# Expert weights loaded in blocks of two experts with 8 KB runs, and multiplied in pairs of blocks

## Chip, core and metric

One core of one Trainium2 chip runs the program. The metric is the device time of one execution in microseconds. The core has five engines with queues of their own: TensorE (PE), VectorE (DVE), ScalarE (ACT), GpSimd (POOL) and SyncE (SP); 16 DMA engines move data between HBM and the on-chip memory. In this kernel SyncE issues all loads of weights. "Records" of a matmul are lines of the trace; one float32 matmul leaves two.

## What is computed

Two blocks of a network over 256 tokens of 1024 features, all in float32. The first block has a mixer (convolution and gated linear attention) and then a mixture of 32 experts; the second block has attention, pooling, a state-space branch and a feed-forward part. The change lies in the mixture of experts of the first block:

```python
def hierarchical_moe(h, w_rg, b_rg, w_re, b_re, w1, w3, w2):
    t = h.reshape(B * S, D)
    lg = (t @ w_rg + b_rg).astype(jnp.float32)             # 4 groups of experts
    ...                                                      # best group, its two best experts, weights
    comb = jnp.einsum("tk,tke->te", w, jax.nn.one_hot(eid, N_EXPERTS, dtype=jnp.float32))
    y = jnp.zeros((B * S, D), jnp.float32)
    for e in range(N_EXPERTS):
        hid = jax.nn.silu(t @ w1[e]) * (t @ w3[e])
        y = y + comb[:, e:e + 1] * (hid @ w2[e]).astype(jnp.float32)
    return y
```

`w1` and `w3` are [32, 1024, 512], `w2` is [32, 512, 1024]: together 201 MB of float32, each read once.

## The kernel before

**Stages.** The program goes through the first block (to about 363 us), the experts (to about 884 us) and the second block. In the stages around the experts the matmuls of L554 and L551 run with split operands made by VectorE and ScalarE; they aren't touched.

**Experts.** They are taken four at a time, eight "quads". For each expert at most `CAP` = 32 tokens are gathered, so the four experts of a quad fill the 128 columns of a tile. The routing (VectorE, with two small steps of ScalarE) makes `hot`, a matrix of ones and zeros; `gather_tokens` (TensorE L803, VectorE L1566) multiplies `uT` (tokens x features) by it and gives `xg`, features on the partitions, in 8 tiles of 128 features. If an expert had more than 32 tokens, a general path (`If_ne`) would run afterwards; it leaves no lines in this trace.

**Blocks and slots.** The weights of a quad come in 12 blocks of 2.097 MB (16 KB on each partition): `wide_of(quad, i)` gives the slot of block i. Blocks 0 to 3 are w1, 4 to 7 are w3, each block two tiles of 128 features for all four experts; blocks 8 to 11 are w2, one tile of 128 hidden features each. There are eight slots (`NW`), three in `above` and five in `arena`, used in turn over all 96 blocks. A row of w1 or w3 is 512 elements, and tiles are taken as `(t p)`: partition p of tile t is feature 128 t + p, so that one contiguous run in HBM is one row, 2 KB (4 KB for w2).

**SyncE.** `expert(quad, i)` (L2463) waits until the slot's former block has been multiplied (`up_made` or `down_made` of that block) and issues four DMAs of 512 KB, one for each expert. The first eight blocks wait for ends of earlier work instead (`out_v`, `scaled_v`). The DMAs of all 96 blocks stand in one row in the queue; the loads of the second block of the network come behind them and wait for `sent[7]`, the end of the last quad on TensorE.

**TensorE, for each quad.** Up products (L825): for w1 and then w3, for each of four blocks, wait for the block (`wide_in`), 2 tiles x 4 experts = 8 matmuls, each expert in its own 32 rows of the bank; `up_made` is raised after each block. Then the gather for the next quad (L803), two transposes of the send weights (L836), four transposes of `hid` (L840), the down products (L849: for each of four blocks 2 x 4 = 8 matmuls, `down_made` after each), and the products that send the results back to the tokens (L862).

**VectorE and ScalarE.** ScalarE makes `s1` = silu of the first bank and copies the transposed `hid` out; VectorE multiplies `s1` by the second bank to `hid`. Ahead of the stage ScalarE copies the turned `u` into `uT` in four pieces (L2135, recorded as L1912).

Of the kernel before, what the change touches and what calls it, by code (L numbers as in the profile page):

```python
# [137 lines left out]
def build(nc, T, out, scratch):  # L138
    ctx = ExitStack()
    with ctx:  # L140
# [274 lines left out]
        w1v, w3v, w2v = (T[n][0].rearrange("(j e) (t p) n -> j p e t n", e=4, p=P) for n in ("w1", "w3", "w2"))  # L415

        def wide_of(quad, i):

            n = 12 * quad + i
            return n % NW, wides[n % NW].rearrange("p (e t n) -> p e t n", e=4, t=2 if i < 8 else 1), n  # L420
# [90 lines left out]
        def tensor_program(e):  # L511
# [298 lines left out]
            for quad in range(8):  # L810
# [5 lines left out]
                for wn in range(2):  # L816
                    bank = take(wn, (silu_a, hid_v)[wn], quad)
                    for th in range(4):
                        s, slot, n = wide_of(quad, 4 * wn + th)
                        e.wait_ge(*wide_in[s][n])  # L820
                        if wn == 0 and th % 2 == 0:
                            e.wait_ge(*gathered[quad, th // 2])
                        for k in range(2):
                            for x in range(4):
                                ins = e.matmul(bank[32 * x:32 * x + 32, :], xg[:, i, 2 * th + k, 32 * x:32 * x + 32],  # L825
                                               slot[:, x, k, :], start=th == 0 and k == 0, stop=th == 3 and k == 1,
                                               skip_group_check=True)
                        ins.then_inc(*up_made.up((quad, 4 * wn + th)))
# [15 lines left out]
                for k in range(4):  # L844
                    s, slot, n = wide_of(quad, 8 + k)
                    e.wait_ge(*wide_in[s][n])
                    for c in range(2):
                        for x in range(4):
                            ins = e.matmul(ob[c][32 * x:32 * x + 32, :], hidT[:, i, k, 32 * x:32 * x + 32],  # L849
                                           slot[:, x, 0, 512 * c:512 * c + 512], start=k == 0, stop=k == 3, skip_group_check=True)  # L850
                    ins.then_inc(*down_made.up((quad, k)))
# [298 lines left out]
        def vector_program(e):  # L1150
            state = dict(split=0, made=0)

            def tt(o, a, b, f):
                return e.tensor_tensor(o, a, b, f)  # L1154
# [416 lines left out]
            for quad in range(8):  # L1571
# [14 lines left out]
                tt(hid, s1, banks[1][:, :], ALU.mult).then_inc(*hid_v.up(quad))  # L1586
# [321 lines left out]
        def scalar_program(e):  # L1908
# [223 lines left out]
            for tc in range(2):  # L2132
                for g in range(2):
                    e.wait_ge(*u_turned[tc, g])
                    act(uT[:, tc, 512 * g:512 * g + 512], bank_of(uT_out, (tc, g))[:, :], ACT.Copy).then_inc(*uT_out.up((tc, g)))  # L2135
# [230 lines left out]
        def sync_program(e):  # L2366
# [83 lines left out]
            def expert(quad, i):  # L2450
                s, slot, n = wide_of(quad, i)
                if n >= NW:
                    prior, pi = (n - NW) // 12, (n - NW) % 12
                    e.wait_ge(*(up_made[prior, pi] if pi < 8 else down_made[prior, pi - 8]))
                elif s < 4:
                    e.wait_ge(*out_v["w_out", 3])
                else:
                    e.wait_ge(*ada_sum[31])
                    e.wait_ge(*scaled_v[1, 6])
                    e.wait_ge(*scaled_a[1, 7])  # L2460
                src, at, kt = (w1v, 2 * i, 2) if i < 4 else (w3v, 2 * i - 8, 2) if i < 8 else (w2v, i - 8, 1)
                for x in range(4):
                    e.dma_start(slot[:, x, :, :], src[quad, :, x, at:at + kt, :]).then_inc(*wide_in[s].up(n, 16))  # L2463
# [128 lines left out]
```

## Time and profile before

| | us |
|---|---|
| median of 3 runs | 1522.9 (1517.42 to 1524.58) |
| profiled execution | 1524.56 |
| its span, first to last instruction | 1522.8 |
| TensorE busy | 1248.3 (82%) |
| VectorE busy | 676.4 (44%) |
| ScalarE busy | 454.5 (30%) |

The share of busy time of an engine is an average over stages that have different limits. The page also splits the span into 40 slices of 38 us with the GB/s that the DMA engines moved in each. The mean granted clock of TensorE is 0.892 of full speed (2.4 GHz; the other level is 1.2 GHz, shown as 0.5). A DMA share of 1 means that packets took all the time of 16 DMA engines; as the records of packets overlap a little, it can read 1.05.

### The profile page before, as it was taken

What the parts mean: (1) busy time and instruction counts of PE and PEld (TensorE: products, weight loads), DVE (VectorE), ACT (ScalarE), POOL (GpSimd) and SP (SyncE); (2) the same over time, 40 slices, a digit from 0 to 9 for tenths busy, and PEclk for the clock granted to TensorE, in tenths of its full rate; (3) what the DMA queues carried; (4) which work ended last, traced back from release to release, by engine and by line L of the source; (5) the groups of instructions that cost most, each with busy time, mean ns of one, the idle gap of its engine ahead of it and who ended that gap; (6) DMA issues with size and microseconds to landing.
All of it is one profiled execution on the core that took longest, in us unless ns stands there. A gap on an engine that the chain in (4) does not pass through costs nothing.

```text
span 1522.8 us, 20505 instructions
## 1 busy us (share of the span) xinstructions
PE 1248.3 (82%) x8742; PEld 970.9 (64%) x8742; DVE 676.4 (44%) x1137; ACT 454.5 (30%) x647; POOL 1.9 (0%) x15
## 2 busy tenths in 40 slices
PE   6889988698676566566757669999999989899998
PEld 3679987587432131221212149989998879899986
DVE  2546985453300000000000055355567777667975
ACT  1533341533100000000000044343444544455453
POOL 0000000000000000000000000000000000000000
PEclk8899989899697887987778689989999989999999
DMA  9686730587999999999999947444346334445652
GB/s 356 240 281 216 220 99 1 198 279 263 391 394 398 387 398 391 395 398 388 399 389 396 396 158 229 152 139 124 126 128 191 112 111 152 136 142 174 200 206 85
DMA packets 226568, 374.51 MB, mean 246 GB/s; under 512 B 8854, under 2 KB 121896, under 8 KB 226344
## 3 DMA queue, kind: packets, MB, share of 16 engines
q1 hardware_dynamic: 226304, 369.58, 68.6%
q0 software_dynamic: 144, 3.54, 0.7%
q8 instruction: 71, 1.16, 0.3%
q14 instruction: 25, 0.20, 0.0%
q10 hardware_dynamic: 24, 0.03, 0.0%
HBM read 372.03 MB, written 4.62 MB: 247 GB/s over the span
## 4 chain that ended last, share of the span: by engine, by line
PE 50%; SPq 22%; DVE 13%; DMA 8%; ACT 3%; issue 3%; DVEq 0%; ACTq 0%
PE bank L554 30%; SPq L2463 22%; DVE arena L1162 5%; DMA arena<-in_w 4%; PE bank L1131 4%; DVE fine L1154 4%; DMA above<-in_w 2%; DVE arena L1154 2%; PE bank L825 2%; ACT fine L1912 2%; DMA arena<-in_w_ada 2%; PE bank L551 2%; PE bank L582 1%; ACT arena L1912 1%; PE bank L751 1%
## 5 line engine op out<-in xcount | busy, mean ns | idle before, releaser
L554 PE MATMUL bank<-fine 128*128 128x256 f32 x4656 | 587.5, 289 | 34.9 <-DVE fine L1154 24.2
L554 PEld LDWEIGHTS bank<-fine 128*128 128x128 f32 x4656 | 577.6, 197 | 44.3 <-issue 33.9
L1154 DVE TENSOR_TENSOR fine<-arena,fine 128x1024 fp32r<-128x1024 f32 (+1 forms) x257 | 299.3, 1192 | 175.3 <-ACT fine L1912 165.9
L1912 ACT ACTIVATE fine<-arena 128x1024 fp32r<-128x1024 f32 (+2 forms) x279 | 267.0, 984 | 178.7 <-PE bank L554 106.7
L1912 ACT ACTIVATE arena<-bank 128x256 f32<-128x256 f32 (+2 forms) x161 | 73.5, 482 | 606.7 <-PE bank L836 194.2
L825 PE MATMUL bank<-arena 128*32 128x512 f32 x640 | 105.7, 798 | 76.0 <-DMA arena<-in_w 76.0
L1154 DVE TENSOR_TENSOR arena<-arena,bank 128x512 f32<-128x512 f32 x8 | 5.5, 689 | 299.6 <-PE bank L825 299.6
L825 PEld LDWEIGHTS bank<-arena 128*32 128x32 f32 x640 | 20.6, 129 | 154.8 <-DMA arena<-in_w 103.1
L1912 ACT ACTIVATE arena<-arena 128x512 f32<-128x512 f32 (+6 forms) x94 | 63.3, 702 | 171.1 <-DVE arena L1154 80.4
L1162 DVE SCALAR_TENSOR_TENSOR arena<-arena 128x256 f32<-128x256 f32 (+2 forms) x265 | 108.3, 481 | 1.2 <-ACT arena L1912 0.8
L825 PE MATMUL bank<-above,arena 128*32 128x512 f32 x384 | 61.7, 778 | 39.5 <-DMA above<-in_w 39.5
L1154 DVE TENSOR_TENSOR arena<-arena 128x512 f32<-128x512 f32 (+5 forms) x138 | 84.1, 633 | 8.6 <-ACT arena L1912 6.7
L1154 DVE TENSOR_TENSOR arena<-bank,arena 128x256 f32<-128x256 f32 (+6 forms) x88 | 36.0, 446 | 86.3 <-PE bank L594 17.0
L849 PE MATMUL bank<-arena 128*32 128x512 f32 x320 | 50.5, 768 | 27.7 <-DMA arena<-in_w 24.2
L825 PEld LDWEIGHTS bank<-above,arena 128*32 128x32 f32 x384 | 12.3, 127 | 86.3 <-DMA above<-in_w 48.1
L1131 PE MATMUL bank<-fine 128*128 128x512 f32 x264 | 60.3, 390 | 0.0
L1598 DVE COPY arena<-bank 128x512 f32<-128x512 f32 x8 | 5.5, 692 | 122.1 <-PE bank L849 122.1
L1131 PEld LDWEIGHTS bank<-fine 128*128 128x128 f32 x264 | 49.4, 188 | 10.7 <-DVE fine L1154 0.3
L849 PEld LDWEIGHTS bank<-arena 128*32 128x32 f32 x320 | 11.0, 131 | 62.1 <-DMA arena<-in_w 36.9
L551 PE MATMUL bank<-fine 128*128 128x256 f32 x384 | 47.1, 283 | 0.1
L551 PEld LDWEIGHTS bank<-fine 128*128 128x128 f32 x384 | 46.4, 192 | 0.3 <-issue 0.3
L803 PEld LDWEIGHTS bank<-arena 128*128 128x128 f32 x256 | 32.7, 211 | 11.7 <-issue 11.7
(160 smaller groups left out, 814.0 us busy)
## 6 DMA issues: line engine op xcount, KB each, us to landing
arena<-in_w SPq DMA_DIRECT2D x240, 512.0 KB, 11.7
above<-in_w SPq DMA_DIRECT2D x144, 512.0 KB, 11.4
arena<-in_w_in SPq DMA_DIRECT2D x62, 1024.0 KB, 5.3
arena<-in_w_ada SPq DMA_DIRECT2D x24, 1024.0 KB, 7.7
arena<-in_ffn_w_up SPq DMA_DIRECT2D x22, 1024.0 KB, 5.1
arena<-in_ffn_w_down SPq DMA_DIRECT2D x11, 1024.0 KB, 4.9
arena<-in_w_ada_f SPq DMA_DIRECT2D x8, 1024.0 KB, 10.6
arena<-in_w_gla_o SPq DMA_DIRECT2D x4, 1024.0 KB, 8.5
```

The lines of the kernel that those rows point to most:

```text
L551: ins = e.matmul(o, x[:, kt, j * P:j * P + P], w[:, k, :], start=start, stop=stop, skip_group_check=True)
L554: ins = e.matmul(o, w[:, k, j * P:j * P + P], x[:, kt, :], start=start, stop=stop, skip_group_check=True)
L582: ins = e.matmul(bank[32 * k:32 * k + 32, :], cact[:, kt:kt + 1].to_broadcast([P, 32]), slot[:, k, :], start=f % 2 == 0, stop=f % 2 == 1, ...
L751: ins = e.matmul(bank[:, j * 256:j * 256 + 256], w_pw[m // 4][:, k, (m % 4) * P:(m % 4) * P + P], sig[:, k, :], start=k == 0, stop=k == 3)
L803: ins = e.matmul(bank[:, j * P:j * P + P], uT[:, tc, k * P:k * P + P], hot2[:, tc, quad * P:quad * P + P], start=tc == 0, stop=tc == 1)
L825: ins = e.matmul(bank[32 * x:32 * x + 32, :], xg[:, i, 2 * th + k, 32 * x:32 * x + 32], slot[:, x, k, :], start=th == 0 and k == 0, stop=t ...
L849: ins = e.matmul(ob[c][32 * x:32 * x + 32, :], hidT[:, i, k, 32 * x:32 * x + 32], slot[:, x, 0, 512 * c:512 * c + 512], start=k == 0, stop ...
L1131: ins = e.matmul(obs[tc][c][:, :], x, w[:, cs], start=n == i == 0, stop=n == 21 and i == 2, skip_group_check=True)
L1154: return e.tensor_tensor(o, a, b, f)
L1162: return e.scalar_tensor_tensor(out=o, in0=a, scalar=s, in1=b, op0=f1, op1=f2)
L1912: return e.activation(o, i, f, bias=bias, scale=scale)
L2463: e.dma_start(slot[:, x, :, :], src[quad, :, x, at:at + kt, :]).then_inc(*wide_in[s].up(n, 16))
```

## The change

The tiles of w1, w3 and w2 are taken as `(p t)`: partition p of tile t is feature 8 p + t for w1 and w3, and hidden feature 4 p + t for w2. Then successive tiles of one partition are neighbours in HBM. A block holds two experts instead of four, and four tiles instead of two (two instead of one for w2), so that a run is 4 x 2 KB or 2 x 4 KB, 8 KB in both cases. The block is as large as before, and there are as many of them; SyncE issues two DMAs of 1 MB for each, one for each expert. The products of four tiles for all four experts need two blocks now, so TensorE waits for both blocks of a pair, runs 16 matmuls and raises `up_made` (or `down_made`) once. Slots are freed likewise, both after the pair. The number of matmuls and their shapes are unchanged.

The features have to be in the same order in the other operand: ScalarE writes `uT` permuted, reading the bank with a stride of 8 elements, and VectorE writes `hid` permuted with a stride of 128 elements.

```diff
--- before.py
+++ after.py
@@ -412,12 +412,14 @@
 
         GENERAL = [i for i in range(NW) if i != 4]
         NG = len(GENERAL)
-        w1v, w3v, w2v = (T[n][0].rearrange("(j e) (t p) n -> j p e t n", e=4, p=P) for n in ("w1", "w3", "w2"))
+        w1v, w3v, w2v = (T[n][0].rearrange("(j e) (p t) n -> j p e t n", e=4, p=P) for n in ("w1", "w3", "w2"))
 
         def wide_of(quad, i):
 
+
+
             n = 12 * quad + i
-            return n % NW, wides[n % NW].rearrange("p (e t n) -> p e t n", e=4, t=2 if i < 8 else 1), n
+            return n % NW, wides[n % NW].rearrange("p (e t n) -> p e t n", e=2, t=4 if i < 8 else 2), n
 
         def general_of(e0, i):
             n = 96 + 3 * e0 + i
@@ -815,17 +817,20 @@
                     e.reg_load(reg, idxb[0:1, 16:17])
                 for wn in range(2):
                     bank = take(wn, (silu_a, hid_v)[wn], quad)
-                    for th in range(4):
-                        s, slot, n = wide_of(quad, 4 * wn + th)
-                        e.wait_ge(*wide_in[s][n])
-                        if wn == 0 and th % 2 == 0:
-                            e.wait_ge(*gathered[quad, th // 2])
-                        for k in range(2):
+                    for th in range(2):
+                        slots = []
+                        for pair in range(2):
+                            s, slot, n = wide_of(quad, 4 * wn + 2 * th + pair)
+                            e.wait_ge(*wide_in[s][n])
+                            slots.append(slot)
+                        if wn == 0:
+                            e.wait_ge(*gathered[quad, th])
+                        for k in range(4):
                             for x in range(4):
-                                ins = e.matmul(bank[32 * x:32 * x + 32, :], xg[:, i, 2 * th + k, 32 * x:32 * x + 32],
-                                               slot[:, x, k, :], start=th == 0 and k == 0, stop=th == 3 and k == 1,
+                                ins = e.matmul(bank[32 * x:32 * x + 32, :], xg[:, i, 4 * th + k, 32 * x:32 * x + 32],
+                                               slots[x // 2][:, x % 2, k, :], start=th == 0 and k == 0, stop=th == 1 and k == 3,
                                                skip_group_check=True)
-                        ins.then_inc(*up_made.up((quad, 4 * wn + th)))
+                        ins.then_inc(*up_made.up((quad, 4 * wn + 2 * th + 1)))
                 if quad == 0:
                     ada_to_mod(15)
                 if quad < 7:
@@ -841,14 +846,19 @@
                 ins.then_inc(*hid_turned.up(quad))
                 ob = [take(2 + n, (expert_a, expert_v)[n], ("ye", quad)) for n in range(2)]
                 e.wait_ge(*hidT_out[quad])
-                for k in range(4):
-                    s, slot, n = wide_of(quad, 8 + k)
-                    e.wait_ge(*wide_in[s][n])
-                    for c in range(2):
-                        for x in range(4):
-                            ins = e.matmul(ob[c][32 * x:32 * x + 32, :], hidT[:, i, k, 32 * x:32 * x + 32],
-                                           slot[:, x, 0, 512 * c:512 * c + 512], start=k == 0, stop=k == 3, skip_group_check=True)
-                    ins.then_inc(*down_made.up((quad, k)))
+                for th in range(2):
+                    slots = []
+                    for pair in range(2):
+                        s, slot, n = wide_of(quad, 8 + 2 * th + pair)
+                        e.wait_ge(*wide_in[s][n])
+                        slots.append(slot)
+                    for k in range(2):
+                        for c in range(2):
+                            for x in range(4):
+                                ins = e.matmul(ob[c][32 * x:32 * x + 32, :], hidT[:, i, 2 * th + k, 32 * x:32 * x + 32],
+                                               slots[x // 2][:, x % 2, k, 512 * c:512 * c + 512], start=th == k == 0,
+                                               stop=th == k == 1, skip_group_check=True)
+                    ins.then_inc(*down_made.up((quad, 2 * th + 1)))
                 e.wait_ge(*send_out[quad])
                 for m in range(8):
                     if quad == 0 and m % 2 == 0:
@@ -1583,7 +1593,8 @@
                 e.wait_ge(*up_made[quad, 7])
                 if quad:
                     e.wait_ge(*hid_turned[quad - 1])
-                tt(hid, s1, banks[1][:, :], ALU.mult).then_inc(*hid_v.up(quad))
+                tt(hid.rearrange("p (t a) -> p a t", t=4), shaped(s1, P, 4), shaped(banks[1][:, :], P, 4), ALU.mult).then_inc(
+                    *hid_v.up(quad))
                 if quad < 7:
                     gather_tokens(quad + 1)
                 e.wait_ge(*route["hot"])
@@ -2132,7 +2143,8 @@
             for tc in range(2):
                 for g in range(2):
                     e.wait_ge(*u_turned[tc, g])
-                    act(uT[:, tc, 512 * g:512 * g + 512], bank_of(uT_out, (tc, g))[:, :], ACT.Copy).then_inc(*uT_out.up((tc, g)))
+                    act(shaped(uT[:, tc, :], 8, P)[:, :, 64 * g:64 * g + 64],
+                        bank_of(uT_out, (tc, g))[:, :].rearrange("p (a t) -> p t a", t=8), ACT.Copy).then_inc(*uT_out.up((tc, g)))
             for tc in range(2):
                 t = rt[:, 128 * tc:128 * tc + 128]
                 e.wait_ge(*route["ex", tc])
@@ -2451,16 +2463,16 @@
                 s, slot, n = wide_of(quad, i)
                 if n >= NW:
                     prior, pi = (n - NW) // 12, (n - NW) % 12
-                    e.wait_ge(*(up_made[prior, pi] if pi < 8 else down_made[prior, pi - 8]))
+                    e.wait_ge(*(up_made[prior, pi | 1] if pi < 8 else down_made[prior, pi - 8 | 1]))
                 elif s < 4:
                     e.wait_ge(*out_v["w_out", 3])
                 else:
                     e.wait_ge(*ada_sum[31])
                     e.wait_ge(*scaled_v[1, 6])
                     e.wait_ge(*scaled_a[1, 7])
-                src, at, kt = (w1v, 2 * i, 2) if i < 4 else (w3v, 2 * i - 8, 2) if i < 8 else (w2v, i - 8, 1)
-                for x in range(4):
-                    e.dma_start(slot[:, x, :, :], src[quad, :, x, at:at + kt, :]).then_inc(*wide_in[s].up(n, 16))
+                src, at, kt = (w1v, 4 * (i // 2), 4) if i < 4 else (w3v, 4 * (i // 2) - 8, 4) if i < 8 else (w2v, 2 * (i // 2) - 8, 2)
+                for x in range(2):
+                    e.dma_start(slot[:, x, :, :], src[quad, :, 2 * (i % 2) + x, at:at + kt, :]).then_inc(*wide_in[s].up(n, 16))
 
             for quad in range(8):
                 if quad == 4:
```

On TensorE, at the start of quad 0 (`wide_in0` to `wide_in7` are the arrivals in the eight slots, `gathered` is `xg`), there stood before:

```order
L825 MATMUL bank<-above,arena 32x512 [waits gathered,wide_in0,pieces_out_by_vector]
L825 MATMUL bank<-above,arena 32x512 x7
L825 MATMUL bank<-above,arena 32x512 [waits wide_in1]
L825 MATMUL bank<-above,arena 32x512 x7
L825 MATMUL bank<-above,arena 32x512 [waits gathered,wide_in2]
L825 MATMUL bank<-above,arena 32x512 x7
L825 MATMUL bank<-arena 32x512 [waits wide_in3]
L825 MATMUL bank<-arena 32x512 x7
```

and now:

```order
L830 MATMUL bank<-above,arena 32x512 [waits wide_in1,gathered,wide_in0,pieces_out_by_vector]
L830 MATMUL bank<-above,arena 32x512 x15
L830 MATMUL bank<-above,arena 32x512 [waits gathered,wide_in3,wide_in2]
L830 MATMUL bank<-above,arena 32x512
L830 MATMUL bank<-arena 32x512 x2
L830 MATMUL bank<-above,arena 32x512 x2
```

Eight matmuls behind one arrival have become sixteen behind two; the second pair has one block in `above` and one in `arena`, so its matmuls alternate between them.

On SyncE, at blocks 6 to 9 (`expert_up` is `up_made`), before:

```order
L2463 DMA arena<-in_w 128x2x512 [waits scaled_by_scalar,scaled_by_vector,ada_sum]
L2463 DMA arena<-in_w 128x2x512 x3
L2463 DMA above<-in_w 128x1024 [waits expert_up]
L2463 DMA above<-in_w 128x1024 x3
L2463 DMA above<-in_w 128x1024 [waits expert_up]
```

and now:

```order
L2475 DMA arena<-in_w 128x2048 [waits scaled_by_scalar,scaled_by_vector,ada_sum]
L2475 DMA arena<-in_w 128x2048
L2475 DMA above<-in_w 128x2048 [waits expert_up]
L2475 DMA above<-in_w 128x2048
L2475 DMA above<-in_w 128x2048 [waits expert_up]
```

Four DMAs of a block have become two, each with one contiguous row of 2048 elements for a partition; the waits stand in the same places, and that of block 8 is for the first pair instead of the first block.

## Rows read from the trace of the kernel before

**Rows 1.** The page, 40 slices of the span: GB/s.

```profile
GB/s 356 240 281 216 220 99 1 198 279 263 391 394 398 387 398 391 395 398 388 399 389 396 396 158 229 152 139 124 126 128 191 112 111 152 136 142 174 200 206 85
```

**Rows 2.** Windows in the expert stage; the header names the columns.

```profile
core 0: us, PE busy (x) PEld busy (x) DVE busy (x) ACT busy (x) POOL busy (x), PEclk, DMA share, GB/s
366.00:408.00 42.00, 25.79 (x139) 22.49 (x141) 20.52 (x81) 9.46 (x19) 0.00 (x0) 0.63 1.05 388
...
440.00:470.00 30.00, 19.04 (x105) 4.53 (x104) 0.00 (x0) 0.60 (x1) 0.00 (x0) 0.72 1.05 386
415.00:430.00 15.00, 12.90 (x114) 7.36 (x110) 3.09 (x8) 0.98 (x2) 0.00 (x0) 0.97 1.03 408
...
728.70:792.50 63.80, 42.62 (x247) 16.16 (x247) 3.09 (x5) 2.18 (x4) 0.00 (x0) 0.73 1.04 394
```

**Rows 3.** Waits, 360 to 890 us: total us, times, longest.

```profile
PE bank L825 <- DMA arena<-in_w: 76.0, 30, 3.6
...
PE bank L825 <- DMA above<-in_w: 39.5, 17, 3.9
```

**Rows 4.** Waits of SyncE over the whole span.

```profile
SPq L2463 <- PE bank L825: 22.8, 10, 7.6
```

**Rows 5.** Timeline, SyncE's issues at the start of the stage: start, us, what.

```profile
363.84 11.03 SPq L2463 DMA_DIRECT2D above<-in_w  x12
374.91 26.39 SPq L2463 DMA_DIRECT2D arena<-in_w  x20
408.96 5.57 SPq L2463 DMA_DIRECT2D above<-in_w  x12
```

**Rows 6.** Timeline, TensorE at the start of the stage.

```profile
401.33 5.71 PE L803 MATMUL bank<-arena 128*128 128x128 f32 x32 [3.54 <-issue]
406.97 5.36 PE L825 MATMUL bank<-above,arena 128*32 128x512 f32 x48
```

**Rows 7.** DMA view, 440 to 470 us (first factors): all packets.

```profile
DMA packets 6008, 11.59 MB, mean 386 GB/s; under 512 B 355, under 2 KB 355, under 8 KB 6007
```

**Rows 8.** DMA view, 415 to 430 us (second factors): all packets.

```profile
DMA packets 1675, 6.12 MB, mean 408 GB/s; under 512 B 184, under 2 KB 184, under 8 KB 1674
```

**Rows 9.** DMA view, 54 to 56 us: constants with rows of 5.25 KB, and others.

```profile
DMA packets 240, 0.82 MB, mean 412 GB/s; under 512 B 28, under 2 KB 69, under 8 KB 240
```

**Rows 10.** DMA view, 370 to 371 us: queue: packets, MB, share of 16 engines.

```profile
q14 instruction: 1, 0.01, 2.1%
```

**Rows 11.** DMA view, 158 to 169.5 us: the copy from scratch to scratch.

```profile
q0 software_dynamic: 139, 3.54, 94.5%
```

**Rows 12.** Chain of waits, 700 to 800 us: start, us, what.

```profile
728.67 2.82 PE bank L825 x16
...
792.50 1.97 PE bank L825 x16
```

**Rows 13.** Timeline, TensorE on two blocks of quad 4.

```profile
643.00 1.92 PE L825 MATMUL bank<-above,arena 128*32 128x512 f32 x16 [1.91 <-DMA above<-in_w]
648.43 3.64 PE L825 MATMUL bank<-arena 128*32 128x512 f32 x16 [3.51 <-DMA arena<-in_w]
```

**Rows 14.** Timeline, TensorE at the end of the stage.

```profile
882.05 1.93 PE L849 MATMUL bank<-arena 128*32 128x512 f32 x16 [1.77 <-DMA arena<-in_w]
884.78 3.69 PE L862 MATMUL bank<-arena 128*128 128x256 f32 x16 [0.81 <-ACT arena L1912]
```

**Rows 15.** Timeline, ScalarE: last of four copies to `uT`, and what follows.

```profile
387.14 0.60 ACT L1912 ACTIVATE arena<-bank 128x512 f32<-128x512 f32 x1 [0.26 <-PE bank L786]
387.76 1.28 ACT L2139 ACT_TABLE_LOAD   x1
```

**Rows 16.** The page: queue (packets, MB, share), issues (count, KB, us to landing).

```profile
q14 instruction: 25, 0.20, 0.0%
...
arena<-in_w SPq DMA_DIRECT2D x240, 512.0 KB, 11.7
...
arena<-in_consts SPq DMA_DIRECT2D x1, 672.0 KB, 10.8
```

## Prediction

> **What bounds the kernel now.** I read the slices of the page first, for the stretch in which the change lies. From about 380 to 870 us the slices stand at 387 to 399 GB/s [rows 1], the highest and flattest stretch of the program; the windows put the DMA share there at 1.03 to 1.05 of 16 engines, with VectorE and ScalarE almost idle and TensorE busy 42.6 of 63.8 us of one quad [rows 2]. This is the expert stage, and its 96 blocks of 2.097 MB are 201 MB. Second, the waits: what TensorE waits for in it is the DMA of the expert weights, some 3.5 us at a time [rows 3]. Third, whether the DMA queue ever waits for a free slot: SyncE waited 22.8 us in all on L825, in 10 waits, the longest 7.6 us [rows 4], and that longest one is the gap between the last issue of the first 32 (374.91 + 26.39 = 401.30) and 408.96 [rows 5]. So the stage is bound by the DMA engines, and the rest of the program (before 365 us and after 884 us) isn't touched, but for shifting.
>
> The period of a quad is 792.50 - 728.67 = 63.83 us in the chain [rows 12]. It has two speeds in it: 386 GB/s while first factors come in (runs of 2 KB) and 408 GB/s while second factors come in (runs of 4 KB) [rows 2]. All have 512 KB in a DMA [rows 16]; what differs is the run.
>
> **Cost of a packet.** From 440 to 470 us 6008 - 355 - 1 = 5652 packets of 2 KB moved [rows 7]: 30 us x 16 / 5652 = 84.9 ns each. From 415 to 430 us 1675 - 184 - 1 = 1490 packets of 4 KB moved [rows 8]: 161.1 ns each. A fixed part c and a part in proportion to the bytes give c = 2 x 84.9 - 161.1 = 8.7 ns, and for 8 KB 2 x 161.1 - 8.7 = 313.5 ns, if a run of 8 KB is one packet. A block is 64, 32 or 16 packets on each engine: 5.43, 5.16 and **5.02 us** (418 GB/s). Check of the old numbers: 8 x 5.43 + 4 x 5.16 = 64.1, against 63.83 in the chain. Nearest row above 4 KB: from 54 to 56 us, while constants with rows of 5.25 KB come in among others, the mean is 412 GB/s [rows 9, 16].
>
> The Trainium skill (DMA: Bandwidth & Descriptors, "Why small descriptors are slow (HBM only)") has a fixed overhead of about 3 cycles per packet, and under "Where 436 GB/s comes from" a ceiling of 435 GB/s. The 8.7 ns above are of that kind, and somewhat more than its 3 cycles at the 850 MHz that the section gives (an estimate of 3.5 ns); by the page's terms an 8 KB block would be about 4.88 us.
>
> **The change part by part.**
> - First factors, 64 blocks: 5.43 to 5.02 us each. Second factors, 32 blocks: 5.16 to 5.02 us. DMAs 384 to 192, so SyncE issues less; it wasn't the limit, since it issued 20 in 26.39 us [rows 5], 5.3 us for the four of a block, in step with a queue that was full. Worth nothing.
> - **The start takes part of it back.** Eight slots are filled while TensorE is still at the routing. The first issue is at 363.84 [rows 5], and from 366 on the rate is full [rows 2]; I take 365.2 as the start, 1.3 us from issue to flow. Before, eight blocks last to 365.2 + 8 x 5.43 = 408.6, and block 8 is issued at 408.96, when block 0 has been multiplied: no gap. The change fills the slots by 365.2 + 8 x 5.02 = 405.4, but L825 begins at 406.97 whatever the DMA does, since it follows the gather of L803 [rows 6] and that the routing. Now both blocks of a pair must be multiplied before a slot is free. 48 records take 5.36 us [rows 6], so 32 take 3.5 and SyncE can issue at about 410.7; data flow again at 412.0. The DMA idles from 405.4 to 412.0, and block 8 starts 412.0 - 408.7 = **3.3 us later** than before. What the faster transfer gained on blocks 0 to 7 is lost here.
> - Blocks 8 to 95: before 56 x 5.43 + 32 x 5.16 = 469.2 us, after 88 x 5.02 = 441.8 us: **27.4 us saved**.
> - Steady stage: the wait for a pair holds the even slot for one block longer, 5 us, and the work on a pair is 3.9 us at 2.4 GHz or 7.3 at 1.2 GHz (1.92 and 3.64 us for 16 records [rows 13]). When a pair has landed, three pairs are queued behind it, 30 us of transfers. TensorE's longest lag behind a landing, all at 1.2 GHz, comes after the last up pair: 7.3 of up, 5.7 of gather [rows 6], 3 of transposes (an estimate), twice 7.3 of down, 7.4 of L862 (twice the 3.69 of rows 14), then the next up pair, 7.3: 45 us after the one landing, and 15 after that of the next up pair, three pairs later. So the queue doesn't run dry: nothing.
> - **The end.** The last block of the stage lands at 882.05 and takes 1.93 us, then come the copies and L862 at 884.78 [rows 14]. Now the last two blocks are multiplied after the landing: 3.9 us at the high clock, 7.3 at the low one, so 1.9 to 5.4 us more. The clock before was mostly between (0.73 of full over a quad [rows 2]); I take the middle, **3.6 us**.
> - uT: four ScalarE copies of 0.60 us, the routing's exponentials right behind them [rows 15]; now they read PSUM with a stride of 8. The trace has no such shape for ScalarE. A gain is excluded, as they would wait for TensorE's transposes all the same; the other bound is twice as long, 4 x 0.60 less 3 x 0.26 of idle time between them = 1.6 us. I take 0, as the elements are as many. Later routing would push the start of L825 and so block 8.
> - hid on VectorE, 0.69 us, is written with a stride: hidden, since the down products wait for their blocks anyway.
>
> **Sum.** 27.4 - 3.3 - 3.6 = 20.5 us less. Against the profiled execution: 1524.6 (span 1522.8) to 1504.1. That execution lies 1.7 us above the median of 1522.9, so the median goes to **1502**.
>
> **Rivals.**
> 1. *No faster than the second factors' runs.* Either the hardware cuts 8 KB rows into 4 KB, or the memory side has its limit at about 408 GB/s. For it: no packet of 8 KB from SyncE is in the trace. Against: the 412 GB/s with rows of 5.25 KB [rows 9]. Then 88 x 5.16 = 454.1, 15.1 us saved, less 6.9: 8 us, **1515**. The skill (HBM Reference, "Specifications (TRN2)") gives about 358 GB/s as effective per core; with that as a cap there would be nothing to win from runs at all. It also says that a core streaming alone measures more, and the trace does: 386 and 408.
> 2. *Slower: a packet of 8 KB costs more than in proportion.* Its place is every block of the stage. Instruction packets have 0.20 MB in 25, 8 KB each [rows 16], and the one amid the stream took 2.1% of 16 us, 336 ns [rows 10]; and packets of 27 KB, copied within HBM, moved 3.54 MB in 94.5% of 11.5 us, 326 GB/s [rows 11]. At 336 ns a block is 5.38 us, 88 are 473.1, 3.9 more than before, and 6.9 on top: 10.8 us more, **1534**. It decides at (469.2 - 6.9) / 88 = 5.25 us a block, 328 ns a packet, 399 GB/s. Against: both are other kinds of transfer, and the first one's time has other packets of the same engine in it (packets of 2 KB overlap likewise: the shares add up to 1.05, not 1). Rows of 8 KB now lie 16 KB apart in HBM, which no row here shows.
> 3. *More than computed.* Without a fixed part at all, 4.88 us a block, and the high clock at the end: 469.2 - 429.4 - 3.3 - 1.9 = 34.6, **1488**.
> 4. *TensorE becomes the bound.* Now 42.6 us of 63.8 are busy at a clock of 0.73 [rows 2]. All at 1.2 GHz a quad is 12 x 3.64 + 5.7 + 7.4 + 3 = 59.8 us [rows 6, 13, 14], against 12 x 5.02 = 60.2 of DMA. It would need that clock in every quad, and then waits between the two could cost some 1 us a quad: about **1510**.
>
> **How the numbers follow.** Forecast 1502, chance 0.62, own range 1495 to 1510 (block 4.95 to 5.07 us, end 1.9 to 5.4, routing 0 to 1.6). Rival 1: 0.15; rival 2: 0.09; rival 3: 0.08; rival 4: 0.06. The range 1490 to 1518 takes in the forecast, rivals 1 and 4 and half of 3; left out are 2 and the rest of 3. A measurement of this kernel tells about 0.5%, 7.6 us, from no change. Rival 1 lies at that bound (1515.3), half of it on either side. Slower is rival 2; same is half of rival 1 and 0.02 of the others' edges: faster 0.81, same 0.10, slower 0.09.
>
> **What would show it.** In the profile after: windows within the stage at 415 to 420 GB/s, equal for first and second factors; quads 60.2 us apart; about 24,600 packets of 8 KB; SyncE's wait before block 8 up from 7.7 us to far more (its 16 DMAs are queued by 380 us), with 0 GB/s between about 406 and 412; L825 in groups of 32 records; the last block landing at about 857 and 3.9 to 7.3 us of work behind it. I'm wrong if the stage stays at 408 GB/s or lower, if L825 begins later than 407, or if the DMA rate falls in the middle of the stage, which would be slots held too long.

## The result

The change brings 1498.4 us (median of 4 runs, 1496.8 to 1502.8) against 1523.7 (4 runs): ratio 0.9847, interval 0.9813 to 0.9881. (Ratios come with 95% intervals; they are not the quotients of the medians shown.) The prediction was 1502, within 1490 to 1518. The profiled execution took 1498.0 us, its span 1496.2.

What answers to [rows 2], windows of the stage after the change (us, busy time of each engine with instructions, granted clock, DMA share, GB/s):

```profile
440.00:470.00 30.00, 16.95 (x98) 4.30 (x96) 0.00 (x0) 0.60 (x1) 0.00 (x0) 0.77 1.01 420
416.00:430.00 14.00, 11.71 (x102) 6.86 (x94) 3.46 (x8) 0.98 (x2) 0.00 (x0) 1.00 1.01 421
```

First factors (from 440 us; 386 GB/s before) and second factors (from 416 us; 408 before) come in at one rate. All packets from 440 to 470 us, to compare with [rows 7]:

```profile
DMA packets 1730, 12.61 MB, mean 420 GB/s; under 512 B 192, under 2 KB 192, under 8 KB 192
```

Taking off the 192 short packets, 16 for each DMA of the weights, and one packet of instructions leaves 1730 - 192 - 1 = 1537 packets of 8 KB: 30 x 16 / 1537 = 312.3 ns each. The sum had 313.5. So a row of 8 KB from HBM is one packet, and rival 1 is out.

The start of the stage, SyncE and TensorE, to compare with [rows 5, 6]:

```profile
361.45 3.36 SPq L2475 DMA_DIRECT2D above<-in_w  x6
364.86 13.84 SPq L2475 DMA_DIRECT2D arena<-in_w  x10
408.31 4.25 SPq L2475 DMA_DIRECT2D above<-in_w  x6
```

```profile
398.94 5.74 PE L805 MATMUL bank<-arena 128*128 128x128 f32 x32 [3.53 <-issue]
404.61 4.06 PE L830 MATMUL bank<-above,arena 128*32 128x512 f32 x34
```

The eight slots are all ordered by 378.7 us; then SyncE has nothing to do until 408.31. The windows show the gap that was forecast:

```profile
404.00:406.00 2.00, 2.00 (x23) 0.99 (x25) 0.69 (x1) 0.00 (x0) 0.00 (x0) 1.00 0.62 258
406.00:408.00 2.00, 2.00 (x24) 0.57 (x20) 0.00 (x0) 0.00 (x0) 0.00 (x0) 1.00 0.02 8
408.00:410.00 2.00, 2.00 (x24) 0.65 (x20) 0.00 (x0) 0.00 (x0) 0.00 (x0) 1.00 0.46 61
410.00:412.00 2.00, 2.00 (x24) 0.60 (x20) 0.00 (x0) 0.25 (x1) 0.00 (x0) 1.00 0.90 348
```

The DMA engines stand still for about 4 us, where 6.6 were forecast (405.4 to 412.0; why it is shorter stands below), because TensorE is still at the routing and then at the first pair. The end, to compare with [rows 14]:

```profile
851.91 6.12 PE L858 MATMUL bank<-arena 128*32 128x512 f32 x32 [6.26 <-DMA arena<-in_w]
858.84 3.48 PE L872 MATMUL bank<-arena 128*128 128x256 f32 x15 [0.81 <-ACT arena L1923]
```

32 records behind the last landing instead of 16, and most of them at 1.2 GHz: 6.12 us instead of 1.93.

SyncE's waits for slots, to compare with [rows 4]; the second row had no counterpart among those shown of before:

```profile
SPq L2475 <- PE bank L830: 73.6, 27, 29.6
...
SPq L2475 <- PE bank L858: 28.0, 11, 5.4
```

It waits 102 us instead of 23, and that costs nothing beyond the start, as the page's GB/s in 40 slices, to compare with [rows 1], stay at 420 or 421 through the middle:

```profile
GB/s 356 267 272 216 218 108 1 197 255 266 367 421 421 421 421 420 421 420 421 421 421 421 297 179 223 127 141 113 129 156 153 139 87 162 134 160 178 197 198 85
```

The queue just holds more. The page has 27.0 us from issue to landing where [rows 16] has 11.7:

```profile
arena<-in_w SPq DMA_DIRECT2D x120, 1024.0 KB, 27.0
above<-in_w SPq DMA_DIRECT2D x72, 1024.0 KB, 26.3
```

**Balance of the two profiled executions.** I count the stage from the first issue of expert weights to the first record of the products after the last block (L862 before, L872 now).

| | before | after | |
|---|---|---|---|
| program start to first issue | 363.84 | 361.45 | -2.4 |
| first issue to issue of block 8 | 45.12 | 46.86 | +1.7 |
| block 8's issue to last landing | 473.09 | 443.60 | -29.5 |
| last work and copies | 2.73 | 6.93 | +4.2 |
| from there to the end of the span | 638.0 | 637.4 | -0.7 |
| span | 1522.8 | 1496.2 | -26.6 |

The stage is 520.9 us before and 497.4 after, **23.5 us shorter**, where 20.5 were forecast; 3 us more lie where both programs do the same. (In another execution of the change, below, the first issue is at 364.54.)

### The profile page after: what moved, and what is told of

It reads as the page before. It is cut to its first block, busy times and chain, and to the rows that moved or that the text cites. A ratio compares the mean times of both kernels' runs of the same rounds, so it can differ in the third digit from the quotient of the medians.

```text
span 1496.2 us, 20337 instructions
## 1 busy us (share of the span) xinstructions
PE 1225.0 (82%) x8742; PEld 974.1 (65%) x8742; DVE 679.2 (45%) x1137; ACT 454.7 (30%) x647; POOL 1.9 (0%) x15
## 4 chain that ended last, share of the span: by engine, by line
PE 55%; DMA 20%; DVE 13%; SPq 5%; ACT 3%; issue 3%; DVEq 0%; ACTq 0%
PE bank L556 30%; DMA arena<-in_w 15%; DVE arena L1172 5%; SPq L2475 4%; PE bank L1141 4%; PE bank L830 4%; DMA above<-in_w 4%; DVE fine L1164 4%; DVE arena L1164 2%; ACT fine L1923 2%; PE bank L858 2%; DMA arena<-in_w_ada 2%; PE bank L553 2%; PE bank L584 1%; ACT arena L1923 1%
## 5 line engine op out<-in xcount | busy, mean ns | idle before, releaser
L830 PE MATMUL bank<-arena 128*32 128x512 f32 x640 | 122.0, 782 | 53.5 <-DMA arena<-in_w 28.8
L1164 DVE TENSOR_TENSOR arena<-arena,bank 128x512 f32<-128x512 f32 x8 | 8.4, 1055 | 277.6 <-PE bank L830 277.6
L830 PE MATMUL bank<-above,arena 128*32 128x512 f32 x384 | 82.5, 786 | 50.8 <-issue 17.9
L830 PEld LDWEIGHTS bank<-arena 128*32 128x32 f32 x640 | 31.0, 138 | 107.5 <-issue 107.5
L830 PEld LDWEIGHTS bank<-above,arena 128*32 128x32 f32 x384 | 21.1, 138 | 108.8 <-issue 108.7
L858 PE MATMUL bank<-arena 128*32 128x512 f32 x320 | 57.0, 742 | 21.7 <-DMA arena<-in_w 19.1
L858 PE MATMUL bank<-above,arena 128*32 128x512 f32 x192 | 34.1, 652 | 20.1 <-DMA arena<-in_w 16.7
L858 PEld LDWEIGHTS bank<-arena 128*32 128x32 f32 x320 | 14.6, 132 | 46.0 <-issue 46.0
```

Source lines behind the costliest of these rows:

```text
L830: ins = e.matmul(bank[32 * x:32 * x + 32, :], xg[:, i, 4 * th + k, 32 * x:32 * x + 32], slots[x // 2][:, x % 2, k, :], start=th == 0 and k ...
L858: ins = e.matmul(ob[c][32 * x:32 * x + 32, :], hidT[:, i, 2 * th + k, 32 * x:32 * x + 32], slots[x // 2][:, x % 2, k, 512 * c:512 * c + 51 ...
```

## Experiments

Each kernel was timed beside the kernel before on the same chip (medians of before 1523.5 to 1524.1), and the ratio is to those runs. "Stage" is counted as above, from each one's profile.

| | median us | ratio to before | stage us | GB/s, 440 to 470 us |
|---|---|---|---|---|
| before | 1523.7 | 1 | 520.9 | 386 |
| the change | 1498.4 | 0.9847 | 497.4 | 420 |
| a_pairs_2k | 1530.3 | 1.0038 [1.0024, 1.0052] | 525.7 | 387 |
| b_4k_single | 1508.4 | 0.9892 [0.9874, 0.9910] | 505.8 | 409 |
| d_16k | 1500.6 | 0.9848 [0.9832, 0.9865] | 497.7 | 427 |
| e_8k_halves | 1896.5 | 1.2473 [1.2402, 1.2544] | 886.9 | 227 |
| i_8k_interleaved | 1500.8 | 0.9856 [0.9834, 0.9877] | 497.9 | 419 |
| f_end | 1496.9 | 0.9832 [0.9814, 0.9849] | 494.3 | 421 |
| g_both | 1494.8 | 0.9808 [0.9794, 0.9822] | 493.2 | 421 |
| h_16k_both | 1487.7 | 0.9755 [0.9739, 0.9770] | 486.1 | 428 |
| j_change_again | 1500.0 | 0.9841 [0.9827, 0.9854] | 497.4 | 420 |
| k_both_again | 1493.7 | 0.9807 [0.9788, 0.9826] | 493.3 | 420 |

### Is it the run, or the pairs with their larger DMAs?

**a_pairs_2k**: the change with the old order of features.

```diff
-        w1v, w3v, w2v = (T[n][0].rearrange("(j e) (p t) n -> j p e t n", e=4, p=P) for n in ("w1", "w3", "w2"))
+        w1v, w3v, w2v = (T[n][0].rearrange("(j e) (t p) n -> j p e t n", e=4, p=P) for n in ("w1", "w3", "w2"))
...
-                    act(shaped(uT[:, tc, :], 8, P)[:, :, 64 * g:64 * g + 64],
-                        bank_of(uT_out, (tc, g))[:, :].rearrange("p (a t) -> p t a", t=8), ACT.Copy).then_inc(*uT_out.up((tc, g)))
+                    act(uT[:, tc, 512 * g:512 * g + 512], bank_of(uT_out, (tc, g))[:, :], ACT.Copy).then_inc(*uT_out.up((tc, g)))
```

(`hid` likewise.)

> The blocks and the pairs of the change, with the old order of features: a block holds two experts and four tiles, two DMAs of 1 MB each, but its runs in HBM are 2 KB (4 KB for w2) as before; uT and hid are not permuted. Theory (the length of the run sets the rate): 386 GB/s for first factors, 408 for second, and only the costs of pairing are left, some 2 to 3 us at the start and 2 to 5 at the end: 5 to 8 us slower than before, about 1529. Rival (half the DMAs, twice as large, and a deeper queue set the rate): 420 GB/s and about the time of the change, 1498 to 1502.

Measured: 1530.3. All packets from 440 to 470 us:

```profile
DMA packets 5841, 11.60 MB, mean 387 GB/s; under 512 B 182, under 2 KB 182, under 8 KB 5840
```

The number of the smallest packets, those that end a DMA, has halved from 355 to 182, and the rate is that of before to 1 GB/s. Half the DMAs at twice the size bring nothing. What is left is the price of pairing: the stage is 4.7 us longer than before, the whole run 6 us.

**b_4k_single**: the new order of features in the old blocks (the lines above the other way round, on the kernel before, with its loads and loops as they were).

> The new order of features in the old blocks: a block holds four experts and two tiles (one for w2), four DMAs of 512 KB, multiplied as soon as it lands; runs are 4 KB for w1, w3 and w2 alike. Theory (8.7 ns a packet and 75.8 for each 2 KB): 5.16 us a block everywhere, 408 GB/s; 56 blocks x 0.27 = 15.1 us saved, some 1.5 lost at block 8, nothing at the end: 13.6 faster than before, about 1510. Rival (nothing happens below 8 KB, or the number of DMAs counts): 386 GB/s, 1523.

Measured: 1508.4. From 440 to 470 us:

```profile
DMA packets 3373, 12.28 MB, mean 409 GB/s; under 512 B 378, under 2 KB 378, under 8 KB 3372
```

3373 - 378 - 1 = 2994 packets of 4 KB, 160.3 ns each (161.1 in the sum). The run alone, in the old blocks, takes 15.1 us off the stage, where 13.6 were expected: from block 8's issue to the last landing it is 456.7 us instead of 473.1, and the last work takes 1.3 us more. That the run and not the order of the rows in HBM does it, the second factors of before show: they had 4 KB runs in the old order, and 161.1 ns a packet [rows 8]. So of the 23.5 us, 15 come with the step to 4 KB, which needs no pairs at all. The step from there to 8 KB adds 8.4: by the packets 88 x (32 x 160.3 - 16 x 312.3) ns = 11.7 us for blocks 8 to 95, less what pairing costs at the ends (4.7 us in a_pairs_2k). These two make 7.0; the other 1.4 us I can't place.

**d_16k**: one expert with all its tiles in a block, 16 KB runs, four blocks multiplied together.

```diff
-            return n % NW, wides[n % NW].rearrange("p (e t n) -> p e t n", e=2, t=4 if i < 8 else 2), n
+            return n % NW, wides[n % NW].rearrange("p (e t n) -> p e t n", e=1, t=8 if i < 8 else 4), n
...
+                    slots = []
+                    for x in range(4):
+                        s, slot, n = wide_of(quad, 4 * wn + x)
+                        e.wait_ge(*wide_in[s][n])
+                        slots.append(slot)
...
-                    e.wait_ge(*(up_made[prior, pi | 1] if pi < 8 else down_made[prior, pi - 8 | 1]))
+                    e.wait_ge(*(up_made[prior, pi | 3] if pi < 8 else down_made[prior, 3]))
...
+                src = (w1v, w3v, w2v)[i // 4]
+                e.dma_start(slot[:, 0, :, :], src[quad, :, i % 4, :, :]).then_inc(*wide_in[s].up(n, 16))
```

> The run doubled again: a block is one expert with all its tiles, one DMA of 2 MB with 16 KB runs, and blocks are multiplied four at a time. Theory: a packet of 16 KB costs 616 ns, a block 4.93 us (425 GB/s), 5 to 6 us less than the change over blocks 8 to 95, against 3.5 us more at the start (32 matmuls before a slot is free) and about 5 more at the end: 1499 to 1504, no gain over the change. Rival: with only one group of four blocks, 20 us, queued behind the one that has landed, the queue runs dry where the last w3 group is followed by gather, transposes and down products, some 2 to 5 us in each quad: 1515 to 1540 and stretches of 0 GB/s in every quad. Second rival: packets of 16 KB aren't faster per byte than those of 8 KB (420 GB/s): 1505 to 1510.

Measured: 1500.6, as its theory had it. From 440 to 470 us:

```profile
DMA packets 886, 12.81 MB, mean 427 GB/s; under 512 B 104, under 2 KB 104, under 8 KB 104
```

886 - 104 - 1 = 781 packets of 16 KB, 614.6 ns each, and 616 were expected. The four sizes measured, 84.9, 160.3, 312.3 and 614.6 ns, lie on one line: 9.2 ns and 75.7 ns for each 2 KB give 84.9, 160.6, 312.0 and 614.8. The queue doesn't run dry (first rival) either, with 428 GB/s from 430 to 830 us, though SyncE waits far longer for slots:

```profile
SPq L2471 <- PE bank L829: 274.1, 15, 37.4
SPq L2471 <- PE bank L855: 132.3, 7, 24.5
```

But the ends eat the gain: block 8 is issued 50.28 us after the first issue (363.98 to 414.26), and behind the last landing stand 64 records:

```profile
414.26 1.28 SPq L2471 DMA_DIRECT2D above<-in_w  x3
```

```profile
851.69 9.22 PE L855 MATMUL bank<-arena 128*32 128x512 f32 x64 [8.40 <-DMA arena<-in_w]
```

### Does the number of DMAs matter with 8 KB runs?

**e_8k_halves**: each DMA of 1 MB cut in two, by partitions.

```diff
                 for x in range(2):
-                    e.dma_start(slot[:, x, :, :], src[quad, :, 2 * (i % 2) + x, at:at + kt, :]).then_inc(*wide_in[s].up(n, 16))
+                    for r in range(2):
+                        e.dma_start(slot[64 * r:64 * r + 64, x, :, :],
+                                    src[quad, 64 * r:64 * r + 64, 2 * (i % 2) + x, at:at + kt, :]).then_inc(*wide_in[s].up(n, 16))
```

> The change with each DMA of 1 MB cut into two of 512 KB, for partitions 0 to 63 and 64 to 127: runs of 8 KB as in the change, number and size of the DMAs as before. Theory (the run alone): 418 to 421 GB/s and the time of the change, 1497 to 1503. Rival (DMA size or number): the rate falls toward 408 and the time rises by 10 us or more.

Both theories failed: 1896 us, 398 more than the change. From 440 to 470 us:

```profile
DMA packets 1038, 6.82 MB, mean 227 GB/s; under 512 B 207, under 2 KB 207, under 8 KB 207
## 3 DMA queue, kind: packets, MB, share of 16 engines
q1 hardware_dynamic: 1037, 6.80, 102.2%
```

The 16 engines are all busy, but a packet of 8 KB takes 30 x 16 / 830 = 578 ns instead of 312. Neither the run nor the count of DMAs has that effect; what is new is that a DMA fills only partitions 0 to 63 or 64 to 127. The Trainium skill has a rule for it (SBUF — State Buffer, "Door 1: The DMA port swizzle (why `[64,N]` ≈ `[32,N]`)"): a DMA's rate goes by how many of 16 ports its partitions reach, and the range 0 to 63, like 64 to 127, reaches 8. By that the rate would be about half of the 436 GB/s that the same section has for 16 ports, 218 (an estimate); the trace has 227 here and 232 from 500 to 1200 us, close to it but 4 to 6% above. Why it is more, no run shows.

**i_8k_interleaved** tests this: the same 384 DMAs of 512 KB, but even and odd partitions (the lines against e_8k_halves).

```diff
-                        e.dma_start(slot[64 * r:64 * r + 64, x, :, :],
-                                    src[quad, 64 * r:64 * r + 64, 2 * (i % 2) + x, at:at + kt, :]).then_inc(*wide_in[s].up(n, 16))
+                        e.dma_start(slot[r::2, x, :, :],
+                                    src[quad, r::2, 2 * (i % 2) + x, at:at + kt, :]).then_inc(*wide_in[s].up(n, 16))
```

> As e_8k_halves, 384 DMAs of 512 KB with 8 KB runs, but one has the even partitions and the other the odd ones. Theory (e_8k_halves was slow since the lower or upper 64 partitions alone are behind half of the ports; neither the number nor the size of DMAs matters): packets at 313 ns, 420 GB/s, the time of the change, 1497 to 1503. Rival (a DMA over 64 partitions, four packets for an engine, is slow in itself): packets near 576 ns and some 1890 us, as there.

Measured: 1500.8, the time of the change. From 600 to 630 us:

```profile
DMA packets 1921, 12.60 MB, mean 420 GB/s; under 512 B 384, under 2 KB 384, under 8 KB 384
```

So 384 DMAs of 512 KB are as good as 192 of 1 MB, a DMA over 64 partitions is fine, and which 64 it has is what made e_8k_halves slow. The rows that a DMA reads in HBM changed along with the partitions, from neighbours to every other one, and no run separates the two. The change reads the same rows as e_8k_halves at the full rate, which speaks for the partitions; that it goes by ports is what the Trainium skill's rule says, and not shown here.

### What do the two ends cost?

**f_end**: the w2 blocks of the last quad in the old shape (four experts, one tile, 4 KB runs), multiplied one by one.

```diff
+        def single(quad, i):
+            return quad == 7 and i >= 8
...
+                    if single(quad, 8 + 2 * th):
+                        for k in (2 * th, 2 * th + 1):
+                            s, slot, n = wide_of(quad, 8 + k)
+                            e.wait_ge(*wide_in[s][n])
+                            for c in range(2):
+                                for x in range(4):
+                                    ins = e.matmul(ob[c][32 * x:32 * x + 32, :], hidT[:, i, k, 32 * x:32 * x + 32],
+                                                   slot[:, x, 0, 512 * c:512 * c + 512], start=k == 0, stop=k == 3,
+                                                   skip_group_check=True)
```

> The change, but the four w2 blocks of the last quad are loaded as before (four experts, one tile, 4 KB runs) and multiplied one by one. Theory (the end of the change costs 4 us, since two blocks are multiplied behind the last landing): last work 1.9 to 3.6 us instead of 6.1, less 0.6 us for the shorter runs: 2 to 4 us faster than the change, 1495 to 1497. Rival (something else is last there): 1498 to 1499, with L872 as late as before.

Measured: 1496.9, stage 494.3, 3.1 us shorter than that of the change. The last rows of TensorE on blocks:

```profile
846.60 1.93 PE L860 MATMUL bank<-arena 128*32 128x512 f32 x16 [2.54 <-DMA arena<-in_w]
851.65 2.58 PE L860 MATMUL bank<-arena 128*32 128x512 f32 x16 [3.12 <-DMA arena<-in_w]
```

2.58 us behind the last landing instead of 6.12. The total alone would not tell it from the change (1493.5 to 1502.0); the stage does.

**g_both**: f_end, and the first two blocks of w1 likewise (the main lines against f_end; the up products get the loop of single blocks too).

```diff
-            return quad == 7 and i >= 8
+            return (quad == 0 and i < 2) or (quad == 7 and i >= 8)
...
-                    e.wait_ge(*(up_made[prior, pi | 1] if pi < 8 else down_made[prior, pi - 8 | 1]))
+                    e.wait_ge(*(up_made[prior, pi if single(prior, pi) else pi | 1] if pi < 8 else down_made[prior, pi - 8 | 1]))
```

> f_end, and the first two w1 blocks likewise loaded and multiplied one by one, so that the slot of block 8 is free after 8 matmuls instead of 16. Theory: block 8 is issued 1.7 us earlier after the first issue of the stage (45.1 us instead of 46.9), the queue idles that much less, the rest as in f_end: 1.5 us below it, 1493 to 1496. Rival (block 9 or a later one binds, as its slot comes free as late as now): as f_end.

Measured: 1494.8, stage 493.2. Block 8 is issued 45.10 us after the first issue (365.50 to 410.60), as expected to a tenth. The stage gains 1.0 us over f_end, of which the last block's work takes some back (3.33 us against 2.58, another clock), so the 1.7 us arrive.

**j_change_again and k_both_again**, the change and g_both on one chip.

> The change as it is, once more, on the same chip as k_both_again, to compare the two directly. Theory (its two ends cost what the traces of f_end and g_both say): 1497 to 1501, and 3 to 5 us slower than k_both_again. Rival (their difference was that of the chips or of the part ahead of the stage): within 1 us of it.

> g_both once more, beside the change: 1493 to 1497, and 3 to 5 us faster than j_change_again by the theory that the first and the last pair cost 1 and 3 us; within 1 us of it by the rival.

Measured: 1500.0 and 1493.7, 6.4 us apart, more than the 3 to 5 expected (k's runs go from 1491.0 to 1498.0). The spans of the two profiled executions differ by 8.6 us (1499.2 and 1490.6). Of these 4.1 lie in the stage, 497.4 against 493.3, and that is what the two ends cost; 1.6 lie ahead of it. The other 2.9 lie behind it: from the stage's end to the end of the span it is 637.3 us against 634.4, and the first profiles have nearly the same two figures (637.4 with the change, 634.3 with g_both), so it came in both pairs of profiles. It begins right behind the stage: from 12 to 24 us after its end TensorE's granted clock is 0.64 with the change and 0.80 with both ends in the old shape, and 1.3 to 1.5 us are gained by there. The programs are alike from there on. With f_end it is 636.7 us. Which end brings it, and how, no run shows.

**h_16k_both**: d_16k with both ends in the old shape, the four w1 blocks of quad 0 and the four w2 blocks of quad 7 (loads and loops for them as in the kernel before).

```diff
+        def single(quad, i):
+            return (quad == 0 and i < 4) or (quad == 7 and i >= 8)
```

> d_16k (16 KB runs, groups of four blocks), with the w1 blocks of the first quad and the w2 blocks of the last one loaded in the old shape (4 KB runs) and multiplied one by one. Theory: the middle keeps 427 GB/s, block 8 is issued at 45 us after the first issue instead of 50.3, and the last work is 1.9 to 3.6 us instead of 9.2: 5 + 6 us, less 1 us for the 4 KB runs, 10 below d_16k's 1500.6: 1489 to 1492, the fastest so far. Rival (the queue runs dry in the middle once it is ahead, since only one group is queued behind the one that has landed): 1494 to 1499 with windows under 420 GB/s.

Measured: **1487.7**, the fastest of all, ratio 0.9755 to before, 11 to 12 us below the change's two medians, and 1.3 us below the range expected. Against d_16k the stage is 11.6 us shorter, where 10 were expected, and the part behind it 2.2 us (634.8 against 637.0), as in the pair above. From 430 to 830 us, and at the end:

```profile
430.00:830.00 400.00, 238.63 (x1632) 97.93 (x1636) 21.48 (x31) 14.25 (x26) 0.00 (x0) 0.80 1.01 427
```

```profile
848.41 1.93 PE L870 MATMUL bank<-arena 128*32 128x512 f32 x16 [2.02 <-DMA arena<-in_w]
```

427 GB/s over 400 us without a break, so the queue doesn't run dry in the middle, block 8 is issued at 45.15 us, and one single block is left behind the last landing.

## Why the prediction was right, and where it was off

**Right.** The stage is bound by the DMA engines and the length of the run sets their rate (a_pairs_2k against b_4k_single: one part each). The fixed part of 8.7 ns a packet, taken from two rows of the trace before, gave 313.5 ns for 8 KB; 312.3 came. The quad was to take 60.2 us. Of the chain of waits after the change:

```profile
511.61 5.64 PE bank L830 x32
...
692.24 5.79 PE bank L830 x32
...
812.10 5.59 PE bank L830 x32
```

180.63 / 3 = 60.2 and 119.86 / 2 = 59.9. No slot was held too long in the middle, and ScalarE's strided copies to `uT` still take 0.60 us (four in 2.4), so the routing ends at the same distance from the first issue: L805 starts 37.49 us after it, as L803 did before. Block 8 was to be issued 46.9 us after the first issue; it was 46.86.

**The start term was mis-sized.** It had the data of block 8 3.3 us later than before. The new side was right: issue at 46.9 us, data from about 48.2 us after the first issue (the windows have them back between 409 and 410 us). The old side wasn't: it let eight blocks end at 408.6, but they didn't have the queue to themselves. One more load stands ahead of them, and its 1 MB was left out:

```profile
363.43 0.37 SPq L2375 DMA_DIRECT2D arena<-in_w_ada_f  x1
```

It moves in 512 packets of 2 KB (the change, with blocks in packets of 8 KB, has 784 - 272 = 512 packets between 512 B and 8 KB from 361 to 408.31 us), 2.7 us at 84.9 ns on 16 engines. With the eight blocks that makes 8192 + 512 = 8704 packets. The kernel before, from 363 to 411 us:

```profile
DMA packets 9169, 17.76 MB, mean 370 GB/s; under 512 B 517, under 2 KB 517, under 8 KB 9166
```

9169 - 517 - 3 = 8649 of them had moved by 411. So the old blocks lasted to about 411.3, the queue had no gap, and block 8, issued at 408.96, cost no time to start. The data of block 8 are then 48.2 - 47.5 = 0.7 us later after the first issue, not 3.3: 2.6 us more gain. The transfers behind it took 470.8 us (411.3 to 882.05) and 442.3 (409.6 to 851.91), 28.5 less, where 27.4 were forecast: 1.1 more, to which packets of 8 KB 1.2 ns cheaper than in the sum bring 1.7 (16 x 88 of them on each engine) and what is left isn't traced. Together 3.7 us more gain than forecast, the same as by the table above (29.5 - 1.7 = 27.8 against 27.4 - 3.3 = 24.1).

The prediction's own numbers could have shown it: the last block was to land at 412.0 + 441.8 = 853.8 by the one way and at 882.05 - 24.1 = 858.0 by the other, and the text wrote 857. It landed at 851.91, 854.3 on the old clock, as the stage began 2.4 us earlier.

**The end term** was 3.6 within bounds of 1.9 to 5.4; it measured 4.2. In the other profiles with pairs up to the end it is 3.2 (a_pairs_2k), 3.4 (i_8k_interleaved) and 4.1 us (j_change_again). The last pair of the change ran mostly at 1.2 GHz: the granted clock is 0.50 from 852 to 856 us,

```profile
852.00:854.00 2.00, 2.00 (x12) 0.58 (x16) 0.00 (x0) 0.00 (x0) 0.00 (x0) 0.50 0.04 8
854.00:856.00 2.00, 2.00 (x12) 0.46 (x8) 0.00 (x0) 0.00 (x0) 0.00 (x0) 0.50 0.00 0
```

after more than 6 us in which TensorE had waited for data. Together 20.5 + 3.7 - 0.6 = 23.6, the stage's 23.5.

**Rivals.** Rival 1 fell with 420 GB/s. Rival 2 (8 KB packets dearer than in proportion) fell with 312 ns: the 336 ns of the instruction packet was no price for a load of weights. Rival 3's block of 4.88 us isn't reached even with 16 KB (8 x 614.6 ns = 4.92). Rival 4 didn't come: the clock stayed mixed, 0.77 from 440 to 470 us.

**Left open.** The profiled execution took 1498.0 us where 1504.1 was forecast: 3 us of that are the terms above, the other 3 lie outside the stage, 2.4 of them ahead of it and 0.7 behind. In the programs of this study, all alike up to there, the first issue comes between 360.8 and 366.4 us. Why, no run shows.

## What to carry to other kernels

Where loads bind, fit the time of a packet from two stretches with different runs and extrapolate; then reorder the contraction index as `(p t)` so that the tiles of one partition are neighbours in HBM. It cost a permuted operand here, and VectorE's longer write of it was hidden. The first doubling of the run is worth more than the next two together: by the packets a block takes 304 ns less with 4 KB than with 2 KB, then 133 and 80 less with 8 and 16 KB. And it comes without any grouping. Larger groups are paid at the two ends of the stage, before the first slot is free and behind the last landing, so keep small blocks there and large ones in the middle. Count before and after between the same two events of a trace, not a model against a measurement, and count what else stands in the queue.

## What the runs showed of the hardware that I had not expected

- A stream of DMAs of 512 KB, in turn over partitions 0 to 63 and 64 to 127, with 8 KB runs goes at 227 GB/s, 578 ns a packet; over the even and the odd partitions at 420 GB/s.
- VectorE's product to `hid` takes longer when it is written with a stride of 128 elements; ScalarE's copy from PSUM with a stride of 8 elements doesn't. The groups of a_pairs_2k (not permuted) and of the change:

```profile
L1164 DVE TENSOR_TENSOR arena<-arena,bank 128x512 f32<-128x512 f32 x8 | 5.5, 689 | 300.4 <-PE bank L830 300.3
```

```profile
L1164 DVE TENSOR_TENSOR arena<-arena,bank 128x512 f32<-128x512 f32 x8 | 8.4, 1055 | 277.6 <-PE bank L830 277.6
```

689 against 1055 ns. It lies beside the DMA here; on a path that VectorE binds it would have to be in the sum.
- With long runs the queue takes more bytes in advance: issue to landing 11.7 us before, 27.0 after, with the slots full. It goes by the run more than by the size of the DMA: 14.6 us in a_pairs_2k (1 MB, 2 KB runs), 21.6 in i_8k_interleaved (512 KB, 8 KB runs).
